# Attention probabilities scaled by GpSimd instead of ScalarE, weight splits between the heads' steps, due query tiles first, and an earlier start for the third GLU unit

## The reference, cut to what matters

```python
y = jax.nn.gelu(y)                       # S5 output
z = y @ w_glu + b_glu                    # 1024 -> 2048
val, gate = jnp.split(z, 2, axis=-1)
h = h + val * jax.nn.sigmoid(gate)
h = h + mlp(rmsnorm(h))
k, v = split(rmsnorm(h) @ w_kv + b_kv)
q = rmsnorm(h) @ w_q + b_q
# for each block of 128 tokens: its own and the previous block of keys
s = where(valid, q @ k.T / 8, -inf)
m = maximum(max(s), sink)
p = exp(s - m)
denom = sum(p) + exp(sink - m)
o = (p / denom) @ v
h = h + o @ w_o + b_o
h = h + mlp(rmsnorm(h))
out = rmsnorm(h)
```

## Time and profile before

| | |
|---|---|
| median of 3 runs | 1022.09 us (1022.05 to 1022.59) |
| profiled execution | 1023.13 us, its span 1021.3 us |
| TensorE matmuls busy | 998.4 us, 98% |
| VectorE | 822.8 us, 81% |
| ScalarE | 487.4 us, 48% |
| GpSimd | 272.4 us, 27% |
| S5 stage, with its last GLU tile | to about 102 us |
| attention steps | about 552 to 642 us |

### The profile page before, as it was taken

How to read it: one execution, slowest core, us unless ns; L and a number is a source line. 1 busy time by engine, 2 the same in 40 slices (tenths; PEclk the granted TensorE clock), 3 DMA queues, 4 the chain that set the end, 5 groups by cost and what they waited for, 6 DMA issues and landing times.

```text
span 1021.3 us, 16652 instructions
## 1 busy us (share of the span) xinstructions
PE 998.4 (98%) x5850; PEld 823.0 (81%) x5850; DVE 822.8 (81%) x1155; ACT 487.4 (48%) x882; POOL 272.4 (27%) x228
## 2 busy tenths in 40 slices
PE   9889999999999999999999999999999999999996
PEld 4677888888888888888887776888888888888886
DVE  7994488698898988986895776889898898989745
ACT  7863323445345444543421878655455354444421
POOL 8995887400000000030967240010000000001150
PEclk9799999999999999999999999999999999999999
DMA  6114333222412233230333110232222412224012
GB/s 255 37 38 139 127 120 127 79 84 83 165 62 103 102 112 115 82 124 1 104 123 122 50 42 21 86 124 101 103 84 82 159 67 103 91 111 147 21 42 83
DMA packets 31877, 97.53 MB, mean 95 GB/s; under 512 B 10696, under 2 KB 13256, under 8 KB 27984
## 3 DMA queue, kind: packets, MB, share of 16 engines
q1 hardware_dynamic: 31824, 96.83, 27.5%
HBM read 92.36 MB, written 2.10 MB: 92 GB/s over the span
## 4 chain that ended last, share of the span: by engine, by line
PE 85%; DVE 6%; ACT 3%; issue 2%; SPq 1%; POOL 1%; DMA 1%; POOLq 0%; DVEq 0%; ACTq 0%
PE ps L1765 17%; PE ps L1768 9%; PE ps L1786 8%; PE ps L1787 8%; PE ps L1788 8%; PE ps L1725 6%; PE ps L1726 6%; PE ps L1727 6%; PE ps L1668 2%; PE ps L1670 2%; PE ps L1669 2%; DVE act L1084 2%; SPq L391 1%; PE ps L1958 1%; PE ps L1933 1%
## 5 line engine op out<-in xcount | busy, mean ns | idle before, releaser
L453 POOL TENSOR_TENSOR gate_sb<-gate_sb 128x1 f32<-128x1 f32 x50 | 18.2, 365 | 715.0 <-DMA raw<-panels_in 501.8
L1787 PE MATMUL ps<-hid,w_hi 128*128 128x512 f32 x384 | 150.5, 392 | 0.0
L1786 PE MATMUL ps<-hid,w_hi 128*128 128x512 f32 x384 | 150.4, 392 | 0.0
L1788 PE MATMUL ps<-hid,w_lo 128*128 128x512 f32 x384 | 149.6, 390 | 0.0
L711 ACT ACTIVATE s_hi<-w_raw 128x1024 fp32r<-128x1024 f32 (+1 forms) x104 | 87.8, 844 | 98.6 <-PE ps L1768 92.8
L543 POOL TENSOR_TENSOR w_lo<-raw,w_hi 128x1024 fp32r<-128x1024 f32 x52 | 130.2, 2505 | 4.2
L1765 PE MATMUL ps<-hid,s_hi 128*128 128x512 f32 x448 | 121.3, 392 | 0.6 <-ACT acc L775 0.6
L1725 PE MATMUL ps<-hid,w_hi 128*128 128x512 f32 x304 | 120.3, 396 | 0.0
L1726 PE MATMUL ps<-hid,w_hi 128*128 128x512 f32 x304 | 118.6, 390 | 0.0
L1727 PE MATMUL ps<-hid,w_lo 128*128 128x512 f32 x304 | 118.5, 390 | 0.0
L1194 DVE TENSOR_TENSOR s_lo<-w_raw,s_hi 128x1024 fp32r<-128x1024 f32 (+1 forms) x104 | 101.8, 990 | 17.6 <-ACT s_hi L711 9.9
(11 more groups left out here) (275 smaller groups left out, 2047.7 us busy)
## 6 DMA issues: line engine op xcount, KB each, us to landing
raw<-panels_in SPq DMA_DIRECT2D x108, 512.0 KB, 3.3
w_raw<-pairs_in SPq DMA_DIRECT2D x28, 1024.0 KB, 5.5
xy<-xu_in SPq DMA_DIRECT2D x4, 512.0 KB, 7.5
out<-h SPq DMA_DIRECT2D x8, 256.0 KB, 2.1
prm<-prm_in SPq DMA_DIRECT2D x1, 1280.0 KB, 5.6
h<-x_rows_in SPq DMA_DIRECT2D x1, 1280.0 KB, 12.9
h<-x_rows_in SPq DMA_DIRECT2D x1, 768.0 KB, 5.5
dd<-dd_in SPq DMA_DIRECT2D x1, 256.0 KB, 5.6
```

What stands on the lines that cost most here:

```text
L1786: mm(to, w_hi[:, s, w], hid[:, 0, 0, HK * par + k, :], start=(k == 0), stop=False)
L1787: mm(to, w_hi[:, s, w], hid[:, 0, 1, HK * par + k, :], start=False, stop=False)
L1788: last = mm(to, w_lo[:, s, w], hid[:, 0, 0, HK * par + k, :], start=False, stop=(k == HK - 1))
```

## The change

Four edits:

1. `norm_p` leaves ScalarE. GpSimd multiplies the four heads' probabilities of a piece by `rden`, repeated along the row, in one instruction in place of four activations. TensorE's wait in `turn_p` is for one signal of it.
2. GpSimd's splits up to `U_BESIDE` - 1 = `U_Q`+5 run as before; after that GpSimd goes through the 16 pieces, norm_p(Q) for each and one split after each even Q from 0 to 10 (units `U_Q`+6 to `U_O`+3). The rest follows after the last piece.
3. On VectorE the query tiles of the steps 3, 7 and 11 are made ahead of `maxima(Q)`, right behind `denominators(Q-1)`. Those of the steps 1, 5 and 9 stay where they were.
4. In the S5 stage the first four k tiles of unit 2 run between `rest_y(7)` and the eighth tile of units 0 and 1; unit 3's first four tiles follow, and the last four of both as a pair.

```diff
+U_BESIDE = U_Q + KT - 2
@@ gpsimd
-            for u in range(3, NU):
+            for u in range(3, U_BESIDE):
+                if not by_vector(u):
+                    split(u)
+
+            def norm_p(Q):
+                n, r = Q % NBLK, Q % DEEP
+                pool.wait_ge(rden_done, Q + 1)
+                p = s_sb[:, r, :, window(n)]
+                tt(p, p, rden[:, r].unsqueeze(2).to_broadcast([P, 4, len(halves_of(n)) * BLK]), mul).then_inc(p_norm, 1)
+
+            for Q in range(QUADS * NBLK):
+                norm_p(Q)
+                if Q % 2 == 0 and U_BESIDE + Q // 2 < U_SIDE:
+                    split(U_BESIDE + Q // 2)
+            for u in range(U_SIDE, NU):
                 if not by_vector(u):
                     split(u)
@@ scalar
-            def norm_p(Q):
-                u, n, r = Q // NBLK, Q % NBLK, Q % DEEP
-                a.wait_ge(rden_done, Q + 1)
-                for j in range(4):
-                    act_fn(s_sb[:, r, j, window(n)], s_sb[:, r, j, window(n)], ACT.Copy,
-                           scale=rden[:, r, j:j + 1]).then_inc(p_norm, 1)
-            skewed([(norm_p, 1), (o_hi, 3), (turned, 2), (exps, 0), (next_pair, None)])
+            skewed([(o_hi, 3), (turned, 2), (exps, 0), (next_pair, None)])
@@ vector
-            def next_queries(Q):
-                if Q % 2 == 0 and 2 + Q // 2 < KT:
+            def next_queries(Q, due):
+                if Q % 2 == 0 and 2 + Q // 2 < KT and (Q % NBLK == NBLK - 2) == due:
                     queries(2 + Q // 2)
+
+            def due_queries(Q):
+                next_queries(Q, True)
+
+            def later_queries(Q):
+                next_queries(Q, False)
-            skewed([(sinks, 0), (denominators, 1), (maxima, 0), (next_queries, 1), (turned, 2), (o_low, 3),
+            skewed([(sinks, 0), (denominators, 1), (due_queries, 1), (maxima, 0), (later_queries, 1), (turned, 2), (o_low, 3),
                     (next_pair, None)])
@@ tensor
             rest_y(NO - 1)
+            paired(U_GLU + 2, 2, hid[:, 0], (y_lo, 1), range(0, 4), of=(0,))
             paired(U_GLU, 0, hid[:, 0], (y_lo, 1), range(KT - 1, KT))
-            paired(U_GLU + 2, 2, hid[:, 0], (y_lo, 1))
+            paired(U_GLU + 2, 2, hid[:, 0], (y_lo, 1), range(0, 4), of=(1,))
+            paired(U_GLU + 2, 2, hid[:, 0], (y_lo, 1), range(4, KT))
@@ tensor, turn_p
-                pe.wait_ge(p_norm, 4 * Q + 4)
+                pe.wait_ge(p_norm, Q + 1)
```

## The result

The changed kernel takes 1023.86 us (median of 17 executions, 1022.8 to 1025.39), the kernel before beside it 1021.97 (17 executions, 1021.64 to 1023.2): the ratio is 1.0013, with an interval of 1.0007 to 1.0019. By the ratio the kernel became 0.13% slower, less than 0.2%; the two medians stand 1.89 us apart, which is 0.18% and the upper end of that interval. The forecast was 1023.5 with a range of 1020.8 to 1025.2. The profiled execution took 1024.6 us, span 1022.8.

The account below looks back on a forecast made before the run. TensorE, busy 998.4 of 1021.3 us, was taken as the bound. GLU -0.96 and attention +2.37 summed to +1.4 us, taking the median from 1022.09 to 1023.5, range 1020.8 to 1025.2.

Parts of the forecast that it names:

- The GLU edit: End of the S5 stage: moved matmuls cover the wait for ScalarE's copy; gain 0.96 us, bounds 0.85 and 0.96.
- The normalization's price: One 128x1024 `norm_p` on GpSimd: 2.0 us taken, upper bound 2.4; a first-block one (n=0) 1.06.
- rival 1: Longer GpSimd normalization of 2.4 us, 0.4 more at each of three attention sites: 1024.7 us; chance 20%.
- The hold: VectorE's SBUF-to-SBUF `qT` write must wait until GpSimd's normalization ends, delaying maxima, exponentials and turned; 1.1 us a site.
- Rival 3: `qT` writes are not held by GpSimd; attention -0.3 us, with GLU -1.2: 1020.9 us; chance 9%.
- Site A: Attention step 3: norm_p(2) makes queries(3) late, so mix(1) starts at 572.4 instead of 570.71: +1.7 us.
- Site B: Attention step 7: norm_p(6) makes queries(5) late, but mix(5) gets 0 more delay, with no slack.
- Site C: Attention step 11: norm_p(10) makes queries(7) late; mix(9) +2.2 us, carried to mix(13) as +2.37.
- step 1: Attention step 1: `qT` write waits for a GpSimd split, so rden(1) comes 0.47 us late, carried to rden(2).

Follow-up runs that it names:

- kernel 2: Changed kernel with the scaled query tile kept in its PSUM bank, so the `qT` write has a PSUM source; 1020.90 us, ratio 0.9989.
- kernel 3: Changed kernel plus five useless matmuls filling TensorE's wait between scores(4) and mix(1); 1023.12 us, ratio 1.001.
- run 4: The changed kernel itself measured again; 1023.26 us, ratio 1.0014; seven executions from 1022.96 to 1023.50, four from 1024.38 to 1025.32.
- kernel 6: Kernel before with only the query tiles of steps 3, 7 and 11 moved ahead of `maxima`, normalization on ScalarE; 1024.65 us, ratio 1.0019.
- kernel 5: Changed kernel with the query tiles of steps 3, 7 and 11 put behind `maxima` again, normalization on GpSimd; 1025.73 us, ratio 1.004.

## Why the prediction was right, and where it was not

**The GLU edit**: forecast -0.96. The gap is gone in the trace, and alone the edit gives 1.15 us by the medians (1021.96 to 1020.81), 0.8 to 1.1 by the traces. Right.

**The normalization's price**: 2.0 taken, 1.89 measured; the bound of 2.4 that rival 1 stood on is out, and so is the estimate of 2.25 from the Trainium skill ("GPSIMD Engine Reference", section 3.1). The n = 0 one took 1.04, forecast 1.06.

**The hold**: right in place and in kind. Three `qT` writes of 1.64 to 1.65 us, each ending 0.28 to 0.29 behind a GpSimd instruction; kernel 2 takes the hold away, and attention falls to 89.44. Rival 3, no hold, had been priced at 1020.9; the kernel in which it holds measures 1020.90. That they are equal is luck, since the parts are off by 0.5 in attention (forecast -0.3, measured +0.18).

The Trainium skill, "SBUF — State Buffer", section "Who interferes with whom", ties the blocking on VectorE's side to certain of its instructions, for TENSOR_SCALAR under conditions on its operands. The trace agrees so far as the write with an SBUF source is held and the one with a PSUM source (0.75 us) is not.

**Site A**: +1.7 forecast; mix(1) comes 20.17 us behind scores(0), before 18.63: +1.54. **Site B**: 0 forecast; mix(5) is at 43.87 against 40.77, +3.10, which is site A and the 1.57 of the clock: 0. **Site C**: +2.2 at mix(9) and +2.37 at mix(13); measured +3.55 and +3.65, less 1.57, which is +1.98 and +2.08. Attention without the clock: 2.04 in the changed kernel and 2.16 in kernel 3, forecast 2.37. Site A is 0.16 under its forecast: the normalization is 0.11 shorter than I took it, and step 1 passed on 0.39 and not 0.47. Site C is 0.22 to 0.29 under.

**What was missing**: the sum had no term for TensorE's clock. I priced a wait at its length, and I had no wait at scores(4), where TensorE stands 0.78 us for the mask addition behind the held write (it ends at 568.14, scores(4) starts at 568.23). In both profiles of the changed kernel the two waits around scores(4) are followed by a stretch at a clock of 0.52 to 0.53, 1.57 us by the rows of the first and 1.45 by kernel 3. For executions without it the forecast of +1.4 is near: the sum by measured terms is -0.96 + 2.1 = +1.1, which on 1022.0 gives 1023.1, where the lower group of run 4 stands. For executions with the low clock this sum is 1.5 short. The median of 1023.86 lies between the two, so its nearness to 1023.5 owes something to luck; in the repetition it was 1023.26. And the 1.04 us by which the profiled execution of before stands above its median, which the prediction gave to both kernels, was that execution's S5 stage (1.26 us later at its last product); it changed nothing in the forecast of the median. The Trainium skill, "TensorE: Matmul & The Clock Gate", Part 1, lets the clock follow how busy TensorE has been and says that the moment of the switch differs between runs of one kernel. The two profiles of the changed kernel agree in the S5 stage: from 30 to 40 us the granted clock is 0.83 in one and 0.52 in the other, from 40 to 50 us 0.83 and 0.97.

**Where the expected gain of the change went**: of what it could win, 0.96 came at the GLU tile. TensorE's wait for `qT` is gone at scores(12), and at scores(4) the one of 0.32 has given way to the 0.78 above; the wait at mix(13) stayed (1.06 before, 1.16 after), and waits of 1.19 and 1.14 are new at mix(1) and mix(9).

## What to carry to other kernels

When work moves to GpSimd, look up what VectorE does in the same microseconds: here a short VectorE instruction from SBUF to SBUF that came late there cost the whole rest of GpSimd's instruction, and giving it a PSUM source cured that (2.0 us of attention between kernels 3 and 2). Ask also what the move is worth once nothing collides: here nothing, until the waits were filled. A wait of TensorE is also a risk for its clock, so name the low clock as a risk of its own (1.5 us here) where two waits stand close together. Fill it with products that are ready, in the amount of the wait: twelve matmuls in three doses won 2.1 us, where whole blocks moved in the same three steps brought new waits of 1.3 and 0.8. And when an effect is smaller than what executions differ by, compare the stage from its own first instruction.

## What the runs showed of the hardware

- A VectorE TENSOR_SCALAR 128x512 from SBUF to SBUF takes 0.49 us alone and 1.65 when GpSimd's 1.89 us TENSOR_TENSOR starts 0.53 ahead of it; the same with a PSUM source takes 0.75 and is not held.
- GpSimd's TENSOR_TENSOR 128x1024 takes 1.89 us with a second operand repeated along the row, and 2.35 to 2.43 with two full ones in the splits of the attention steps.
- The granted clock fell behind waits of 0.78 and 1.19 us that stand 0.72 apart (0.52 and 0.53, in the two profiles of the changed kernel), behind one wait of 1.89 (0.67 over four microseconds, kernel 6) and behind the 2.37 of kernel 5 (0.51; scores of 1.23 in place of 0.71). Behind single waits of 1.14, 1.16, 1.19 and 1.29 us mixes ran in 1.08.
- With the GLU edit in, scores(0) starts at 549.96 in the changed kernel and at 552.17 in kernel 3, though nothing ahead of it differs between the two, which is more than the whole effect. A stretch at the lower clock between 65 and 72 us (0.77 against 1.00) goes with it.
